# Two-unit attention steps in the second block, and new step sequences in all four mixers, in a two-block transformer kernel

## The chip, the cores and the metric

The kernel runs as one program on one core of a Trainium2 chip. The metric is device time in microseconds (us) of one execution, the median of several. TensorE (PE in the rows) multiplies; VectorE (DVE) and ScalarE (ACT) work on rows of 128 partitions; GpSimd (POOL) does little here; SyncE (SP) issues nearly all DMAs, which bring 389 MB of weights from HBM.

## The reference

One sequence of 256 tokens of width 1024, float32, goes through two different blocks of two layers each. A layer is a mixer and then a feed-forward part.

```
# first block, a layer                       # second block, a layer
h = rms_norm(x)*(1+scale)+shift              h = rms_norm(x)
proj = h @ w_in          # 1024 x 3088       proj = h @ w_in            # 1024 x 2656
a = stick_breaking_attention  # 8 heads      y_a = softmax attention, low-rank q, k, v   # 4 heads
b = gla_chunked          # 4 heads           y_b = difference of two softmaxes times v   # 4 heads
x += gate * ([a, b] @ w_out)                 y_c = banded softmax attention with sinks   # 4 heads
x += gate * (32 SwiGLU experts, 2 a token)   y_d = 4 heads with a bias table (na_rpb)
                                             x += [norm y_a, y_b, norm y_c, norm y_d] @ w_out
                                             x += relu(h @ w_up)**2 @ w_down
```

The modulation (scale, shift, gate) of the first block is `silu(c) @ w_ada`, 1024 x 6144 for each layer. In the second block every one of the four branches works on 256 x 256 scores for each head: for the rows of one half i (128 queries), score = q k^T times a scale (with a mask or bias in C and D), softmax over 256 keys, times v of 64 columns. In B the two softmaxes of a head are combined as p0/sum0 - lambda p1/sum1 before the product with v.

## The kernel before

The four mixers are called mix1 (first block, layers 0 and 1) and mix2 (second block). In the profiled execution they lie at about 38 to 194 us, 437 to 579, 825 to 966 and 1151 to 1290. The experts follow each mix1, the feed-forward part (L536, L2335) each mix2.

**Weights.** Weights come by DMA into four slots of 1 MB (`ring`). Most are split into two float32r parts, ACT writing the rounded part (L916) and DVE the rest (L925), in two halves of 1024 columns each. Every product with them is three matmuls (`parts3`). The weights of the modulation and a few small ones are used unsplit.

**Lanes.** Within a mixer each engine's program is woven from several generators, the lanes. `steps(order, *lanes)` goes through a string of digits; each digit advances the lane of that number to its next `yield`. So the string `ORDER[mixer, layer, engine]` is the order in which the engine issues its work, and nothing else decides it. An engine does its instructions in that order and waits at semaphores. A digit whose lane has ended, or is empty, does nothing.

In mix1 the lanes are 0 the projections (`pe_main1`: L516, L536, and the output projection L737), 1 the attention heads in pairs (`pe_heads` lane 0), 2 nothing, 3 the heads one at a time, 4 the gated linear attention (`pe_gla`: L820, L830 to L834, transposes L845), 5 the modulation (`pe_ada_lane`: column sums L597, and where a gate is made the product L608, to which DVE adds the bias with L625), 6 the transposes of q and k (L759). In mix2 they are 0 the projections (`pe_main2`, L1780, L1804, output L1828), 1 to 3 the attention units, 4 the rest (`pe_misc2`), and on ACT and DVE 5 and 0 for the splits and the projections' evacuation.

**Units.** There are 20 attention units in a mix2: (branch, query half i, part p), 8 of B, 4 each of A, C and D. Each has two score rows (j = 0, 1), 128 x 256 each, in one PSUM bank (2 KB a partition). They are dealt in turn to three lanes with one bank each (3, 4, 5). On PE a unit has three steps: scores S (L1850, two matmuls), transposes T of the probabilities (L1859), product V with v (L1865). Between S and T, DVE finds the row maxima (L2151) and negates and scales them (L2158), in C and D after adding mask or bias (L2149); ACT takes the exponentials, one instruction for each score row (L1992); B also divides and combines on DVE (L2165 to L2170). Between T and V, ACT copies the transposed probabilities out of PSUM (L1998). After V, DVE moves the result to `y` (L2175, L2178), which also frees the bank for the lane's next S. S of B, C and D contracts over 64 partitions or fewer: part p's operands lie in partitions 0 to 63 or 64 to 127, by p. A contracts over 96.

**Fins.** After the last unit of a branch, `pe_fin2` (L1944) transposes its normed y, ACT and DVE turn it into two parts (L2068, L2256), and the output projection L1828 of that tile can run. The order of tiles there is B, A, C, D.

## Time and profile before

| | |
|---|---|
| median of 3 runs | 1479.4 us (1476.24 to 1483.46) |
| the profiled execution | 1481.0 us, of it 1478.8 us from the first to the last instruction |
| PE busy | 1314.6 us, 89% |
| DVE busy | 730.4 us, 49% |
| ACT busy | 526.9 us, 36% |
| mean granted clock of TensorE | 0.962 of full speed |

Two kinds of stretch alternate. In the experts the DMA engines are busy all the time at 421 GB/s and PE works for about two thirds of it. In the mixers and in the second block's feed-forward part PE is busy nearly all the time and the DMA engines are not. Lines are those of the kernel before; in the listings of the changed kernel they are shifted, L1850 to L1870, L1859 to L1880, L1865 to L1888, L1804 to L1822, L1828 to L1846, L1944 to L1968.

### The profile page before, as it was taken

Reading aid. Unit: us, or ns where it says so; the run is one execution under the profiler, and the core shown is the slowest. Engines: PE = TensorE matmul, PEld = TensorE weight load, DVE = VectorE, ACT = ScalarE, POOL = GpSimd, SP = SyncE. Lnnn points to the kernel's source line nnn. Section 1 sums busy time; section 2 is a strip of 40 time slices with the busy share of each in tenths; the row PEclk is TensorE's granted clock in tenths of the full one; section 3 lists DMA queues with packets and bytes.
Section 4 is the critical chain, followed back from the end, with each engine's and each line's share of the span. In section 5 each row is a group of like instructions: output and inputs, shape, how many; then the busy total and the mean of one; then the engine's idle time right before and its main releaser. Section 6 shows DMA issues by size and latency. Waiting matters only on the chain. (4 is left out here: it accounts for less than half of the span.)

```text
span 1478.8 us, 21544 instructions
## 1 busy us (share of the span) xinstructions
PE 1314.6 (89%) x9066; PEld 981.4 (66%) x9066; DVE 730.4 (49%) x1126; ACT 526.9 (36%) x894; POOL 50.7 (3%) x46
## 2 busy tenths in 40 slices
PE   5999998766579999976666999999999999999997
PEld 2765674433247667633432778789898878799986
DVE  1744653121146467321111777765555777764554
ACT  3535331000044354200000546654444546644343
POOL 0200000000002000000000110000000110000000
PEclk9999999888899999998887999999999999999999
DMA  9798799999977957999999714456555305455551
GB/s 353 284 334 308 280 413 421 421 421 420 399 283 275 341 200 301 421 421 421 421 393 402 179 32 172 142 156 202 186 193 173 107 3 198 143 168 189 186 198 43
DMA packets 135976, 392.10 MB, mean 265 GB/s; under 512 B 26816, under 2 KB 40128, under 8 KB 111296
## 3 DMA queue, kind: packets, MB, share of 16 engines
q1 hardware_dynamic: 132128, 389.48, 70.7%
q10 hardware_dynamic: 3744, 1.15, 0.4%
q8 instruction: 76, 1.25, 0.3%
q14 instruction: 28, 0.23, 0.0%
HBM read 389.45 MB, written 1.05 MB: 264 GB/s over the span
## 5 line engine op out<-in xcount | busy, mean ns | idle before, releaser
L413 DVE TENSOR_TENSOR spl<-ring,spl 128x2048 fp32r<-128x2048 f32 x65 | 149.3, 2297 | 135.7 <-ACT spl L404 135.7
L536 PEld LDWEIGHTS ps<-hh,spl 128*128 128x128 f32 x1728 | 204.1, 189 | 6.9 <-issue 5.8
L536 PE MATMUL ps<-hh,spl 128*128 128x256 f32 x1728 | 206.2, 280 | 2.8 <-DVE hh L499 2.8
L404 ACT ACTIVATE spl<-ring 128x2048 fp32r<-128x2048 f32 x66 | 126.7, 1920 | 148.3 <-PE ps L536 107.7
L2335 PE MATMUL ps<-spl,ur 128*128 128x512 f32 x768 | 176.7, 389 | 0.0
L2335 PEld LDWEIGHTS ps<-spl,ur 128*128 128x128 f32 x768 | 143.2, 188 | 29.2
L925 DVE TENSOR_TENSOR spl<-ring,spl 128x1024 fp32r<-128x1024 f32 (+2 forms) x120 | 138.4, 1175 | 24.6 <-ACT spl L916 24.2
L1337 PE MATMUL ps<-ring,ar 128*32 128x256 f32 x928 | 98.5, 443 | 57.4 <-issue 25.0
L1337 PE MATMUL ps<-spl_as_slots,ar 128*32 128x256 f32 x864 | 103.8, 479 | 45.1 <-DMA spl_as_slots<-in_w_up 29.3
L916 ACT ACTIVATE spl<-ring 128x1024 fp32r<-128x1024 f32 (+2 forms) x120 | 116.8, 1011 | 49.4 <-DMA ring<-in_w_out 11.7
L516 PE MATMUL ps<-spl,hh 128*128 128x512 f32 x480 | 117.6, 398 | 3.8 <-DVE spl L925 1.3
L1550 DVE TENSOR_TENSOR ar<-ps,ar 128x256 f32<-128x256 f32 x16 | 6.8, 425 | 223.9 <-ACT ar L1426 223.9
L1337 PEld LDWEIGHTS ps<-ring,ar 128*32 128x32 f32 x928 | 49.9, 127 | 93.5 <-issue 82.3
L516 PEld LDWEIGHTS ps<-spl,hh 128*128 128x128 f32 x480 | 88.4, 188 | 32.1 <-issue 12.3
L1426 ACT ACTIVATE ar<-ps 128x256 f32<-128x256 f32 x16 | 6.2, 385 | 283.6 <-PE ps L1337 283.6
L1337 PEld LDWEIGHTS ps<-spl_as_slots,ar 128*32 128x32 f32 x864 | 51.7, 136 | 70.1 <-issue 62.2
L1804 PE MATMUL ps<-hh,spl 128*128 128x256 f32 (+1 forms) x672 | 85.9, 286 | 3.0 <-DVE hh L499 2.9
L1804 PEld LDWEIGHTS ps<-hh,spl 128*128 128x128 f32 (+1 forms) x672 | 81.6, 192 | 7.0 <-issue 4.1
L597 PE MATMUL ps<-ring,ccol 128*32 128x512 f32 x384 | 53.4, 652 | 18.0 <-DMA ring<-in_w_ada 15.7
L1382 PE MATMUL ps<-spl_as_slots,ar 128*32 128x512 f32 x400 | 58.1, 594 | 10.6 <-ACT ar L1439 6.6
L1402 PE MATMUL ps<-gate,hh_as_floats 128*128 128x512 f32 x128 | 63.0, 614 | 1.9 <-ACT hh_as_floats L1435 1.7
L1329 PE MATMUL ps<-ar,xn 128*128 128x256 f32 (+1 forms) x320 | 58.3, 340 | 0.0
(370 smaller groups left out, 1758.5 us busy)
## 6 DMA issues: line engine op xcount, KB each, us to landing
ring<-in_w_up SPq DMA_DIRECT2D x52, 1024.0 KB, 5.3
spl_as_slots<-in_w_down SPq DMA_DIRECT2D x50, 1024.0 KB, 15.4
ring<-in_w_ada SPq DMA_DIRECT2D x48, 1024.0 KB, 7.2
spl_as_slots<-in_w_up SPq DMA_DIRECT2D x40, 1024.0 KB, 17.4
ring<-in_w_gate SPq DMA_DIRECT2D x38, 1024.0 KB, 16.8
ring<-in_w_down SPq DMA_DIRECT2D x38, 1024.0 KB, 4.9
ring<-in_w_in SPq DMA_DIRECT2D x34, 1024.0 KB, 7.5
ring<-in_w_out SPq DMA_DIRECT2D x16, 1024.0 KB, 6.9
```

The source lines that it names most:

```text
L404: sc.activation(t.hi, t.raw, ACT.Copy).then_inc(s_hi, 2)
L413: v.tensor_tensor(t.lo, t.raw, t.hi, ALU.subtract).then_inc(s_lo, 1)
L516: ins = pe.matmul(ps[:, banks[i], 0:cn], le, ri, start=(kk == 0 and q == 0), stop=(kk == 7 and q == 2), skip_group_check=True)
L536: ins = pe.matmul(ps[:, banks[m // 2], (m % 2) * 256:(m % 2) * 256 + 256], le, ri, start=(kk == 0 and q == 0 and m % 2 == 0), stop=(kk == ...
L916: sc.activation(t.hi[:, h], t.raw[:, h], ACT.Copy).then_inc(s_hi, 1)
L925: ins = v.tensor_tensor(t.lo[:, h], t.raw[:, h], t.hi[:, h], ALU.subtract)
L1329: ins = pe.matmul(slots_out(c, k), xn[:, i, 128 * k:128 * k + 128], mo.pr[:, i, s0:s0 + n], start=(i == 0), stop=(i == 1), skip_group_chec ...
L1337: ins = pe.matmul(ps[32 * j:32 * j + 32, 2 + q % 2, 256 * z:256 * z + 256], mo.xg[:, e // 16, k, 32 * (e % 16):32 * (e % 16) + 32], T[("ga ...
L1382: ins = pe.matmul(ps[32 * j:32 * j + 32, c, :], mo.aT[q % 2][:, f, 32 * j:32 * j + 32], T["down", l, 4 * q + j].raw[:, f, 512 * c:512 * c ...
L1402: pe.matmul(ps[:, 6 + m % 2, :], mo.pT[:, q, 128 * i:128 * i + 128], mo.ys[:, 512 * c:512 * c + 512], start=True, stop=True).then_inc(s_b, 1)
L1804: ins = pe.matmul(o, le, ri, start=(kk == 0 and q == 0 and m % 2 == 0), stop=(kk == 7 and q == 2), skip_group_check=True)
L2335: ins = pe.matmul(ps[:, 2 * cc + i, :], le, ri, start=(d == 0 and f2 == 0 and f == 0 and q == 0), stop=(d == 7 and f2 == 1 and f == 1 and ...
```

## The change

The three unit lanes of mix2 become two. Lane 1 has seven double units, each of both parts of one branch and half (two of B's four), with two PSUM banks (3 and 4). Lane 3 (bank 5) has six single units. Together they hold the same 20 parts. A double unit's instructions are the same matmuls and exponentials, one for each part; what DVE and ACT can do over both parts at once becomes one instruction of twice the width: the maxima (1024 columns instead of 512), the small operations on sums, C's mask, the copy after T and the evacuation after V. In B's combination and D's bias there is still one instruction for each part. The score matmuls are written with j outside and the part a inside, so that neighbours lie in different halves of the partitions.

```diff
-        UNITS = [Unit(br, i, p) for br, n in (("B", 4), ("A", 2), ("C", 2), ("D", 2)) for p in range(n) for i in range(2)]
...
-                self.b, self.units = 3 + z, UNITS[z::3]
...
-        LANES = [Lane(z) for z in range(3)]
+        LANES = [Lane(0, units_of(("B", 0, (0, 1)), ("B", 1, (0, 1)), ("B", 0, (2, 3)), ("A", 0, (0, 1)), ("C", 0, (0, 1)), ("D", 0, (0, 1)),
+                                  ("D", 1, (0, 1)))),
+                 Lane(1, units_of(("B", 1, (2,)), ("B", 1, (3,)), ("A", 1, (0,)), ("A", 1, (1,)), ("C", 1, (0,)), ("C", 1, (1,))))]
...
-                for j, (q, k) in enumerate(u.qk):
-                    ins = pe.matmul(ps[:, L.b, 256 * j:256 * j + 256], q, k, start=True, stop=True)
+                for j in range(2):
+                    for a in range(len(u.ps)):
+                        q, k = u.qk[a][j]
+                        ins = pe.matmul(ps[:, L.b + a, 256 * j:256 * j + 256], q, k, start=True, stop=True)
...
-                for j in range(2):
-                    ins = sc.activation(L.pt[:, j, :], src[:, j, :], ACT.Exp, bias=sm[:, j:j + 1], scale=1.0 if masked else u.scale,
-                                        accum_out=sm[:, 2 + j:3 + j])
+                for a in range(L.n):
+                    for j in range(2):
+                        m = 2 * a + j
+                        ins = sc.activation(L.pt[:, a, j, :], src[:, a, j, :], ACT.Exp, bias=top[:, m:m + 1], scale=1.0 if masked else u.scale,
+                                            accum_out=total[:, m:m + 1])
...
+                elif u.br == "D":
+                    for a, p in enumerate(u.ps):
+                        ins = v.scalar_tensor_tensor(L.pt[:, a, :, :], src[:, a, :, :], scale, na_bias(p, u.i), ALU.mult, ALU.add)
...
-                v.wait_ge(*own_dve(v.tensor_reduce(sm[:, 0:2], src, AX.X, ALU.max)))
+                v.wait_ge(*own_dve(v.tensor_reduce(pair(top), src, AX.X, ALU.max)))
```

All strings of `ORDER` are new, those of mix1 too, where nothing else changes and where the digit 2 is gone:

```diff
-ORDER = {("mix1", 0, "PE"): "004004000665505005566501525301535005650051255345025314542012513215205054351045551040454250152550054420030040005", ...
+ORDER = {("mix1", 0, "PE"): "00400400550506655050505660355540515053505401543505515305531003550414555415410055140150004400000", ...
```

What SP and POOL issue, and its order, stays. The places below are those on which the prediction rests.

**PE, end of mix1 layer 0.** L608 makes a half of a gate, L597 is the next column sum of the modulation, L737 the output projection. Before:

```order
105 L597 MATMUL ps<-ring,ccol 32x512 x4
106 L516 MATMUL ps<-spl,hh 128x512 x12
107 L608 MATMUL ps<-ar,cst 128x512
108 L597 MATMUL ps<-ring,ccol 32x512 x8
109 L737 MATMUL ps<-spl,ur 128x512 x24
```

Changed:

```order
86 L608 MATMUL ps<-ar,cst 128x512
87 L831 MATMUL ps<-xn,ar 128x256
88 L834 MATMUL ps<-ar,xn 128x128 x2
89 L831 MATMUL ps<-xn,ar 128x256
90 L834 MATMUL ps<-ar,xn 128x128 x2
91 L860 MATMUL ps<-ar 128x256 x2
92 L863 MATMUL ps<-ar 128x128 x2
93 L516 MATMUL ps<-spl,hh 128x512 x24
94 L597 MATMUL ps<-ring,ccol 32x512 x8
```

The column sum that stood right behind the gate's product now has other matmuls between.

**PE, middle of mix2 layer 0**, from the last units of B to the first of A. Changed:

```order
1167 L1880 MATMUL ps<-cst,xn 128x128 x4
1168 L1888 MATMUL ps<-ar,xn 128x64 x4
1169 L1870 MATMUL ps<-ar 128x256 x2
1170 L1870 MATMUL ps<-gate,ar 128x256 x2
1171 L1822 MATMUL ps<-hh,spl 128x256 x24
1172 L1935 MATMUL ps<-ar,ring 64x256 x4
1173 L1822 MATMUL ps<-hh,spl 128x256 x24
1174 L1940 MATMUL ps<-ring,ar 128x256 x2
1175 L1880 MATMUL ps<-cst,xn 128x128 x4
1176 L1870 MATMUL ps<-ar 128x256 x2
1177 L1888 MATMUL ps<-ar,xn 128x64 x4
1178 L1870 MATMUL ps<-ar 128x256 x4
```

In rows 1167 to 1169 T, V and the next S of lane 1 stand directly behind one another, and in 1177 and 1178 V and the next S again. Before, in the same place, steps of other lanes stood between two steps of one lane:

```order
1174 L1804 MATMUL ps<-hh,spl 128x256 x12
1175 L1865 MATMUL ps<-ar,xn 128x64 x2
1176 L1859 MATMUL ps<-cst,ar 128x128 x2
1177 L1859 MATMUL ps<-cst,xn 128x128 x2
1178 L1850 MATMUL ps<-ar 128x256
1179 L1850 MATMUL ps<-gate,ar 128x256
1180 L1804 MATMUL ps<-hh,spl 128x256 x24
```

**PE, end of mix2 layer 1**, the last units, of D. Before:

```order
1350 L1850 MATMUL ps<-ar 128x256 x2
1351 L1865 MATMUL ps<-ar,xn 128x64 x4
1352 L1859 MATMUL ps<-cst,ar 128x128 x4
1353 L1828 MATMUL ps<-spl,hh 128x512 x12
1354 L1865 MATMUL ps<-ar 128x64 x4
1355 L1859 MATMUL ps<-cst,xn 128x128 x4
```

Changed:

```order
1315 L1870 MATMUL ps<-ar 128x256 x4
1316 L1846 MATMUL ps<-spl,ur 128x512 x12
1317 L1968 MATMUL ps<-cst,gate 128x128 x4
1318 L1880 MATMUL ps<-cst,xn 128x128 x8
1319 L1846 MATMUL ps<-spl,hh 128x512 x12
1320 L1888 MATMUL ps<-ar,xn 128x64 x8
```

Row 1315 is S of the last double unit and 1318 its T; between them stand 12 matmuls of the output projection and one fin. It is the same in layer 0.

## Rows read from the trace of the kernel before

**Rows 1.** Windows: the mixers and two short stretches; us busy (instructions), clock, DMA.

```profile
core 0: us, PE busy (x) PEld busy (x) DVE busy (x) ACT busy (x) POOL busy (x), PEclk, DMA share, GB/s
38.40:193.60 155.20, 150.28 (x833) 103.82 (x834) 89.15 (x132) 67.71 (x98) 12.49 (x8) 0.99 0.86 308
167.10:170.50 3.40, 3.40 (x15) 1.09 (x8) 2.76 (x4) 2.78 (x3) 0.00 (x0) 0.50 0.38 108
437.50:579.00 141.50, 140.49 (x770) 101.94 (x771) 88.02 (x126) 66.84 (x96) 12.45 (x8) 1.00 0.75 266
824.70:966.40 141.70, 139.38 (x873) 117.77 (x874) 106.23 (x214) 72.84 (x184) 12.01 (x9) 0.98 0.41 126
880.50:883.90 3.40, 3.40 (x16) 2.98 (x15) 3.26 (x6) 1.21 (x4) 2.68 (x2) 0.50 0.00 0
1151.00:1290.40 139.40, 136.55 (x873) 115.09 (x874) 107.67 (x214) 76.15 (x186) 11.08 (x9) 1.00 0.37 119
```

**Rows 2.** Timeline of PE, mix1 layer 0: start, us, line, [idle before <-releaser].

```profile
109.45 2.96 PE L516 MATMUL ps<-spl,hh 128*128 128x512 f32 x12 [1.34 <-DVE spl L925]
113.43 1.06 PE L597 MATMUL ps<-ring,ccol 128*32 128x512 f32 x8 [1.02 <-DMA ring<-in_w_ada]
...
163.10 1.02 PE L608 MATMUL ps<-ar,cst 128*128 128x512 f32 x2
166.45 3.06 PE L597 MATMUL ps<-ring,ccol 128*32 128x512 f32 x16 [2.33 <-DVE gate L625]
```

**Rows 3.** Timeline of PE, pieces of mix1 layer 1 and of mix2 layer 1.

```profile
479.87 0.70 PE L860 MATMUL ps<-ar 64*128 64x256 f32 x4
480.40 0.39 PE L863 MATMUL ps<-ar 64*128 64x128 f32 x4
...
489.38 0.70 PE L860 MATMUL ps<-ar 64*128 64x256 f32 x2
489.92 0.38 PE L863 MATMUL ps<-ar 64*128 64x128 f32 x2
...
1184.31 0.70 PE L1850 MATMUL ps<-ar 64*128 64x256 f32 x2
1184.85 0.59 PE L1850 MATMUL ps<-gate,ar 64*128 64x256 f32 x2
1185.37 0.61 PE L1889 MATMUL ps<-ar 32*32 32x256 f32 x2
...
1243.73 0.61 PE L1859 MATMUL ps<-cst,ar 128*128 128x128 f32 x4
```

**Rows 4.** Waits of PE in mix2 layer 1: us in total, times, longest.

```profile
PE ps L1944 <- DVE gate L2178: 0.6, 1, 0.6
PE ps L1865 <- ACT ar L1998: 0.5, 1, 0.5
PE ps L1859 <- DVE xn L2170: 0.2, 1, 0.2
```

**Rows 5.** Timeline of mix2 layer 1, one unit of D from S to the exponentials.

```profile
1266.04 1.13 PE L1850 MATMUL ps<-ar 64*128 64x256 f32 x4
1267.29 0.69 DVE L2149 SCALAR_TENSOR_TENSOR ar<-ps,ar 128x512 f32<-128x512 f32 x1 [0.84 <-PE ps L1850]
1268.73 0.17 DVE L2158 TENSOR_SCALAR st<-st 128x2 f32<-128x2 f32 x1
1268.94 0.51 ACT L1992 ACTIVATE ar<-ar,st 128x256 f32<-128x256 f32 x1 [0.84 <-DVE st L2158]
```

**Rows 6.** Groups of instructions: busy us, mean ns of one, idle before.

```profile
L1065 DVE TENSOR_REDUCE st<-ar 128x16 f32<-128x1024 f32 x2 | 2.4, 1220 | 2.7 <-ACT ar L944 2.7
L2151 DVE TENSOR_REDUCE st<-ps 128x2 f32<-128x512 f32 x12 | 8.2, 686 | 1.7 <-PE ps L1850 1.6
L916 ACT ACTIVATE spl<-ring 128x1024 fp32r<-128x1024 f32 x18 | 18.5, 1054 | 1.3 <-PE ps L1828 1.3
L1998 ACT ACTIVATE xn<-ps 128x512 f32<-128x512 f32 x8 | 4.8, 594 | 4.2 <-PE ps L1859 4.2
```

**Rows 7.** Timeline of mix2 layer 1: the last V, its evacuation and the fin behind it.

```profile
1280.20 1.00 PE L1865 MATMUL ps<-ar,xn 128*128 128x64 f32 x8
1281.23 0.29 DVE L2178 TENSOR_TENSOR gate<-ps,st 128x128 f32<-128x128 f32 x1 [0.80 <-PE ps L1865]
1281.78 0.63 PE L1944 MATMUL ps<-cst,gate 128*128 128x128 f32 x4 [0.58 <-DVE gate L2178]
```

**Rows 8.** Timeline of PE, the same 96 matmuls at the start of mix2 in layer 0 and layer 1.

```profile
824.78 12.79 PE L1804 MATMUL ps<-hh,spl 128*128 128x256 f32 x96 [2.24 <-DVE hh L499]
1151.12 11.18 PE L1804 MATMUL ps<-hh,spl 128*128 128x256 f32 x96 [0.62 <-DVE hh L499]
```

More of the change, by code:

```diff
@@ L1738, in program, with __init__ @@
-        LANES = [Lane(z) for z in range(3)]
+            def __init__(self, z, units):
+                self.b, self.units, self.n = 3 + 2 * z, units, 2 - z
+                n = self.n
+                self.sm = [st[:, 160 + 24 * z + 2 * n * q:160 + 24 * z + 2 * n * q + 2 * n] for q in range(6)]
+                pt, ptT = ((xn[:, 0, :], xn[:, 1, :]) if z == 0 else (carve(5632, 512), carve(7424, 512)))
+                self.pt = pt.rearrange("p (a j b) -> p a j b", j=2, b=256)
+                self.ptT = ptT.rearrange("p (a j b c) -> p a j b c", j=2, b=2, c=128)
+                self.ptTw = ptT.rearrange("p (a n) -> p a n", n=512)
+                self.banks = ps[:, self.b:self.b + n, :]
+                self.scores = self.banks.rearrange("p a (j n) -> p a j n", n=256)
+                self.psum, self.scalar, self.vector = p_ln[z], a_ln[z], v_ln[z]
@@ new lines, in units_of, with pair @@
+        def units_of(*parts):
+            return [Unit(br, i, p) for br, i, p in parts]
+        LANES = [Lane(0, units_of(("B", 0, (0, 1)), ("B", 1, (0, 1)), ("B", 0, (2, 3)), ("A", 0, (0, 1)), ("C", 0, (0, 1)), ("D", 0, (0, 1)),
+                                  ("D", 1, (0, 1)))),
+                 Lane(1, units_of(("B", 1, (2,)), ("B", 1, (3,)), ("A", 1, (0,)), ("A", 1, (1,)), ("C", 1, (0,)), ("C", 1, (1,))))]
+        def pair(sm):
+            return sm.rearrange("p (a j) -> p a j", j=2)
@@ L1856, in pe_units @@
                     pe.wait_ge(L.scalar, 2 * at + 1)
-                for j in range(len(u.vs)):
-                    for kt in range(2):
-                        ins = pe.transpose(ps[:, L.b, 256 * j + 128 * kt:256 * j + 128 * kt + 128], L.pt[:, j, 128 * kt:128 * kt + 128], ident)
+                for a, vs in enumerate(u.vs):
+                    for j in range(len(vs)):
+                        for kt in range(2):
+                            ins = pe.transpose(ps[:, L.b + a, 256 * j + 128 * kt:256 * j + 128 * kt + 128], L.pt[:, a, j, 128 * kt:128 * kt + 128],
+                                               ident)
                 ins.then_inc(L.psum, 1)
@@ L1862, in pe_units @@
                 pe.wait_ge(L.scalar, 2 * at + 2)
[L1863 to L1865 removed]
+                for a, vs in enumerate(u.vs):
+                    for j, c in enumerate(vs):
+                        for kt in range(2):
+                            ins = pe.matmul(ps[:, L.b + a, 64 * j:64 * j + 64], L.ptT[:, a, j, kt, :], m2.v[:, kt, c:c + 64], start=(kt == 0),
+                                            stop=(kt == 1))
                 ins.then_inc(L.psum, 1)
@@ L1953, in pe_mix2 @@
                 pe_spin(pe, 6, 2)
-            steps(ORDER["mix2", l, "PE"], pe_main2(pe, g, l), *(pe_units(pe, l, L) for L in LANES), pe_misc2(pe, l))
+            steps(ORDER["mix2", l, "PE"], pe_main2(pe, g, l), pe_units(pe, l, LANES[0]), iter(()), pe_units(pe, l, LANES[1]), pe_misc2(pe, l))
         def act_main2(sc, l):
@@ L2079, in act_mix2 @@
             act_hT(sc, g, PR(f"n1{l}"), last, 1)
-            steps(ORDER["mix2", l, "ACT"], act_split(sc, last), *(act_units(sc, l, L) for L in LANES), act_misc2(sc, l), act_main2(sc, l))
+            steps(ORDER["mix2", l, "ACT"], act_split(sc, last), act_units(sc, l, LANES[0]), iter(()), act_units(sc, l, LANES[1]), act_misc2(sc, l), act_main2(sc, l))
             for c in range(2):
@@ L2274, in dve_mix2 @@
             dve_hT(v, g, PR(f"n1{l}"), last, 1)
-            steps(ORDER["mix2", l, "DVE"], dve_split(v, last), *(dve_units(v, l, L) for L in LANES), dve_misc2(v, l), dve_main2(v, l))
+            steps(ORDER["mix2", l, "DVE"], dve_split(v, last), dve_units(v, l, LANES[0]), iter(()), dve_units(v, l, LANES[1]), dve_misc2(v, l), dve_main2(v, l))
             v.wait_ge(s_used, T["out2", l, 2].m + 1)
```

116 lines of the change are left out of this document (62 added, 54 removed), and 6 rows, old and new, of the table ORDER.

## The prediction

> **What bounds the kernel now.** I read the windows first, stage by stage [rows 1]. All that the change touches lies in the four mixers, and in them PE is the limit: it is busy for 150.3 of 155.2 us, 140.5 of 141.5, 139.4 of 141.7 and 136.6 of 139.4. DVE (89 to 108 us) and ACT (67 to 76) have time to spare, so that fewer of their instructions gain nothing by themselves. A gain must come from PE's waits, from PE working on fewer passes one after another, or from the clock. The windows bound the first: the waits of the four mixers are 4.9, 1.0, 2.3 and 2.8 us, 11.0 in all. Next I read in PE's timeline where they are, and how many passes a score step takes.
>
> **Mix1, layer 0.** The largest wait of all is 2.33 us at 166.45: the column sum L597 needs the PSUM bank that L625 on DVE still reads, and it stands directly behind the product L608 that L625 waits for [rows 2]. Changed, that sum stands behind 4 L834, two L831, one pair of heads and 24 L516, some 8 us of PE work, against the 3.35 us from L608's start to the sum's start in the trace. So this wait goes: -2.3. Right behind it the granted clock is 0.50 for 3.4 us, the lower level, 1.2 GHz [rows 1], and the 16 passes of L597 take 3.06 us, where 8 take 1.06 [rows 2]; that is about 1.0 more there, and somewhat more in the L737 behind. What PE did before it: it stood still for those 2.33 us. I take -1.6 with it (bounds 0 and -1.7, half of 3.4). The waits of 1.34 (splits of a late tile) and 1.02 (a tile of modulation weights) [rows 2] come from DMA at 0.86 of its capacity over the stage; the new sequence consumes the same tiles in the same load order, and I leave half of them: -1.2. New waits: L820 stands three times with only about 2 us between (6 us before), and each needs four small DVE operations on the state; I take +1.0 (0 to 2.5). The new place of the last column sums is covered. Sum: -4.1, with the bounds -6.0 and 0.
>
> **Does it reach the end?** Behind this stage the experts run at the DMA's full rate, and one could think that the gain drowns there. The DMA runs at 0.86 in the stage because it waits for slots that PE and the splits free; if these come 4 us earlier, so does all that is queued behind. I let it pass whole except for 0.6. So -3.5.
>
> **Mix1, layer 1.** 1.0 us of waits in all [rows 1]. The new sequence keeps the same neighbours by and large; -0.4, bounds -0.9 and +1.5.
>
> **Mix2, what PE saves.** A score step of a unit (two matmuls in float32, two passes each, hence x4) holds PE from 1184.31 to 1185.37, 1.06 us [rows 3]. Two matmuls whose operands lie in different halves of the partitions run side by side: in mix1 the pair of heads (x4 in L860, x4 in L863) is through in 0.85 us, and a single head (x2, x2) in the same 0.85 [rows 3]. In a double unit of B, C or D the parts lie in different halves, in A they don't (96 partitions). So six of the seven double units save one step of 1.06 us, 6.4 us in a mixer. Against this, the kernel before already has neighbours of this kind: three units' steps stand together at the start of B, and in layer 1 two more in C and D. I take off 1.3 in layer 0 and 2.1 in layer 1: PE saves **5.1 and 4.3 us**. T and V, over 128 partitions, keep their time. If the pairs should not run side by side with two banks as outputs, this is zero; the heads of mix1 write two banks too, so I hold that unlikely.
>
> **Mix2, what PE waits for instead.** With three lanes there were 1.3 to 2.3 us of waits inside each mixer, the longest 0.6 [rows 4]. With two lanes a lane's next step comes sooner, and a double unit takes longer on the way. I price its ways from single rows:
> - S to T in D: 0.2 to reach DVE (S ends about 1267.1, L2149 starts at 1267.29); two L2149 of 0.69; the maxima over 1024 columns 1.22 [rows 5, 6]; L2158 0.2; four exponentials at one in 0.5 us, 1.9; 0.1 back: **5.1 us**. A needs 3.7, B (with its combination) 5.9.
> - T to V: 0.2, a copy of 1024 columns 1.05, 0.05: **1.3 us**; of 512 columns 0.85 [rows 6]. No copy of 1024 out of PSUM is in the trace; L916 of that width is the nearest row, and twice 0.594 the upper bound, 1.4.
> - V to the next S of the lane: 0.74, as from the end of the last V (1281.04) to L1944 at 1281.78 [rows 7]; 0.9 where the evacuation is wider.
>
> Then I add up the PE work that stands between (1.06 a score step, 0.22 a transpose, 2.8 for 12 L1828) and take the difference where it is short. Layer 0: T, V and S of the second double unit of B directly behind each other 0.8 + 0.7; V to S into A 0.9; T to V of A's single unit, directly behind, 0.95; S of A's second single unit, whose evacuation stands behind a split on DVE, 1.1; the fin of B and the first S of A 0.3; T to V of D's first double unit 0.4; V to S of its second 0.9; S to T of the last one, 5.1 against the 3.2 of the fin and 12 L1828 between them, **1.9**; the end as now 0.8. Together 8.7, against 2.3. Layer 1 is laid out more loosely: V to S in B 0.7, S to T in B and A 1.2, V to S in A 0.3, D 0.4 + 0.1 + 1.9, the end and small ones 1.3: 5.9 to 7, against 2.8, so +3.8. So the mixers come to -5.1 + 6.4 = **+1.3** and -4.3 + 3.8 = **-0.5**. Bounds of each: all waits but the 1.9 covered, -3.5; every way longer by a split of 1.2 us in between at three more places, +5.
>
> The Trainium skill bears on this (TensorEngine Tiling (Array Packing), Performance Considerations, PSUM Bottleneck): packing speeds up the matmuls but not the evacuation of PSUM, which may become the bottleneck. By the packing alone the second block would gain the whole 9.4 us; by this rule the gain is spent on waits for ACT and DVE. My ways worked out from the rows side with the rule.
>
> **The clock in mix2.** The same 96 matmuls take 12.79 us in layer 0 and 11.18 in layer 1 [rows 8], and at 880.5 the clock is again 0.50 for 3.4 us although PE was busy all the time [rows 1]. Each such stretch costs up to 1.7. New waits of 1.9 us may bring one more, other positions may spare one; I leave the sum as it is and let the range have 1.7 on both sides. The Trainium skill says the same (TensorE: Matmul & The Clock Gate, Part 1): the point at which the clock changes depends on how the work happens to lie, from run to run.
>
> **Sum.** -3.5 - 0.4 + 1.3 - 0.5 = -3.1 us, against 1481.0 of the profiled execution (span 1478.8 and 2.2 around it): 1477.9. That execution is 1.6 above the median of the three runs, 1479.4; on the median the forecast is **1476 us**.
>
> **Rivals.**
> - The ways are covered (chance 0.22). The waits of mix2 stay at their 5.1 us and the packing pays in full: -9.4 - 3.9 gives **1466**. For it: DVE and ACT lose the fixed cost of many small instructions, the maxima 2 x 686 against 1220 ns [rows 6]. Against it: the last S to T is 1.9 short whatever DVE does.
> - The gain of mix1 is lost, to late tiles or in the experts, and mix2 comes out even (0.20): **1480**.
> - Slower (0.13): the long uninterrupted work of a double unit on DVE (D: 1.38 + 1.22 in a row) stands ahead of the splits L925, and PE's projections wait for their tiles, which they never do inside mix2 now. It decides from about 0.9 us at each of the 12 tiles of a mixer; 1 us at each, in both mixers, is +24, of which some replaces the waits counted above: at half of the tiles +10 to 12, **1487**.
> - The forecast (0.45).
>
> **How the numbers follow.** About 0.5%, 7.4 us, is what a measurement of this kernel can tell from no change: faster is below 1472.0, slower above 1486.8. Faster: the first rival and a fifth of the forecast, 0.31. Slower: half of the last rival and a bit, 0.08. The rest, 0.61, is no change. The range runs from 1466, the first rival, to 1483, with which the upper bounds of the forecast are in and most of the slower rival is out.
>
> **What would show it.** In mix1 layer 0 no wait for L625 at L597, and the stage (38.4 to 193.6) shorter by 3 to 5 us. In mix2, score steps of double units with x8 in about 1.06 us; if they take 2.1, the packing failed and the time is near 1486. A wait of about 1.9 us at the last T of lane 1 in both layers, waits of 0.7 to 1 at V and S of the double units, and stages of 139 to 144 us. If PE's waits in each stay below 3 us, the first rival is right. What would make it wrong altogether is a change outside of the mixers: the experts' stretches should keep their lengths to 2 us.

## The result, and the profile after

The changed kernel takes **1493.0 us** (median of 4 runs, 1489.6 to 1495.1), the kernel before 1479.3: a ratio of 1.0084, with an interval of 1.0065 to 1.0103. It is slower by 0.8%, where the forecast was 1476 with a range up to 1483. The profiled execution is the fastest of the four, 1489.6 us, span 1487.5; that of before took 1481.0. These two traces differ by 8.7 us of span, less than the 12.4 us that the ratio gives, so one pair of traces does not hold the whole loss.

The windows of the changed kernel, the mixers first, in the form of [rows 1]:

```profile
core 0: us, PE busy (x) PEld busy (x) DVE busy (x) ACT busy (x) POOL busy (x), PEclk, DMA share, GB/s
38.10:191.90 153.80, 149.19 (x831) 102.60 (x832) 88.72 (x131) 67.36 (x97) 12.50 (x8) 1.00 0.85 305
436.80:579.50 142.70, 138.90 (x768) 101.25 (x769) 87.81 (x126) 66.36 (x95) 12.82 (x8) 1.00 0.74 260
825.90:972.50 146.60, 137.62 (x872) 116.28 (x873) 98.77 (x179) 71.27 (x173) 10.47 (x9) 0.95 0.39 121
1157.50:1298.80 141.30, 135.40 (x872) 113.80 (x873) 99.75 (x179) 73.45 (x175) 12.29 (x9) 0.98 0.37 118
...
903.90:907.30 3.40, 3.40 (x13) 2.60 (x12) 3.12 (x8) 1.27 (x5) 0.00 (x0) 0.50 0.99 384
...
955.10:958.50 3.40, 3.40 (x10) 2.53 (x9) 1.41 (x2) 1.08 (x3) 0.00 (x0) 0.50 0.00 0
1211.10:1217.90 6.80, 6.42 (x29) 5.40 (x29) 3.19 (x5) 1.53 (x7) 6.04 (x5) 0.50 0.00 0
```

From here on a mixer's length is counted from the start of its first projection matmul to the start of its last matmul of the output product. In the trace of before these lengths are 154.9, 141.2, 141.4 and 139.0 (the windows of [rows 1] are 0.3 to 0.4 wider). Against them the four mixers of the changed kernel are 1.0 shorter, 1.6 longer, 5.2 longer and 2.3 longer; the experts behind mix1 are 0.6 and 0.3 longer, the start is 0.4 shorter, and the rest the same. So the loss in this trace is in mix2. PE is busy there for hardly less than before (137.6 against 139.1, 135.4 against 136.3 on the same bounds), although it does fewer passes one after another. The column of the granted clock says why: 0.95 and 0.98, where [rows 1] has 0.98 and 1.00. Four stretches of 3.4 us in layer 0 and one of 6.8 in layer 1 ran at the lower level, 0.50; before there were two of 3.4 (from 825.9 and from 880.5) and none.

The waits of PE in mix2 layer 0, in the form of [rows 4] (for one line waiting for another: us in total, times, longest):

```profile
PE ps L1846 <- DVE hh L2293: 2.9, 2, 2.7
PE ps L1888 <- ACT ar L2025: 2.8, 1, 2.8
PE ps L1822 <- DVE hh L499: 2.2, 1, 2.2
PE ps L1888 <- ACT xn L2025: 1.0, 2, 0.7
PE ps L1870 <- DVE gate L2211: 0.8, 2, 0.4
```

(The one of 2.2 lies ahead of the stage.) With the shorter ones that are left out here, the waits come to 9.0 us in the stage (146.6 less 137.6), where 2.3 had been; in layer 1 to 5.9, where 2.8 had been. The two long ones, in the timeline of PE, with two rows of ACT for the first:

```profile
899.15 0.60 PE L1880 MATMUL ps<-cst,ar 128*128 128x128 f32 x4
899.63 2.00 ACT L916 ACTIVATE spl<-ring 128x1024 fp32r<-128x1024 f32 x2 [1.54 <-DMA ring<-in_w_in]
901.97 0.58 ACT L2025 ACTIVATE ar<-ps 128x512 f32<-128x512 f32 x1
902.60 1.10 PE L1888 MATMUL ps<-ar 128*128 128x64 f32 x8 [2.84 <-ACT ar L2025]
903.54 0.76 PE L1968 MATMUL ps<-cst,gate 128*128 128x128 f32 x4
904.24 2.08 PE L1870 MATMUL ps<-ar 96*128 96x256 f32 x4
...
948.25 2.08 PE L1870 MATMUL ps<-ar 64*128 64x256 f32 x8 [0.52 <-DVE gate L2214]
950.26 1.11 PE L1968 MATMUL ps<-cst,gate 128*128 128x128 f32 x4
954.05 4.57 PE L1846 MATMUL ps<-spl,hh 128*128 128x512 f32 x12 [2.67 <-DVE hh L2293]
```

At 902.60 V (L1888) of A's first single unit stands directly behind its T (L1880). Its copy L2025 could start at 899.8, when T ends, but ACT has two weight splits and two steps of the fin of B ahead of it, and the splits had themselves waited 1.54 us for a DMA. At 954.05 the output product needs L2293 of the fin of C, which stands on DVE behind the bias and the maxima of the last double unit. At the lower clock matmuls take up to twice their length: L1870 at 904.24, behind the first wait, takes 2.08 us where it takes 1.10 at full clock, and around the second wait L1870 at 948.25 takes 2.08 where it takes 1.13, and 12 L1846 take 4.57 where they take 2.99 a little later. At the second place the clock had fallen at 948.2, before the wait of 2.67 us began.

What the double units were to bring is there. Four rows of the changed kernel, score steps of a double and of a single unit of C and D, in mix2 layer 1:

```profile
1245.66 1.13 PE L1870 MATMUL ps<-ar 64*128 64x256 f32 x8
1246.73 3.10 PE L1798 MATMUL ps<-spl,hh 128*128 128x256 f32 x24
...
1254.35 1.13 PE L1870 MATMUL ps<-ar 64*128 64x256 f32 x4
1255.41 3.00 PE L1846 MATMUL ps<-spl,ur 128*128 128x512 f32 x12
```

Eight passes or four, the next instruction starts 1.06 to 1.07 us later. A's double unit is the comparison: its parts take 96 partitions each and can't lie in different halves, and there eight passes take 1.99 us.

```profile
897.32 1.99 PE L1870 MATMUL ps<-ar 96*128 96x256 f32 x8 [0.38 <-DVE gate L2211]
```

### The profile page after: what moved, and what is told of

Read it like the earlier page. It is cut to its first block, busy times and chain, and to the rows that moved or that the text cites. A ratio compares the mean times of both kernels' runs of the same rounds, so it can differ in the third digit from the quotient of the medians.

```text
span 1487.5 us, 21416 instructions
## 1 busy us (share of the span) xinstructions
PE 1313.9 (88%) x9066; PEld 978.3 (66%) x9066; DVE 715.6 (48%) x1056; ACT 523.4 (35%) x878; POOL 50.8 (3%) x46
## 3 DMA queue, kind: packets, MB, share of 16 engines
HBM read 389.45 MB, written 1.05 MB: 263 GB/s over the span
## 4 chain that ended last, share of the span: by engine, by line
PE 71%; DMA 20%; DVE 4%; ACT 3%; issue 1%; ACTq 0%; SPq 0%; POOL 0%; DVEq 0%
PE ps L536 13%; PE ps L2372 12%; DMA spl_as_slots<-in_w_up 8%; PE ps L1337 6%; PE ps L1822 5%; PE ps L516 5%; PE ps L1382 4%; DMA spl_as_slots<-in_w_down 4%; PE ps L1846 3%; DMA ring<-in_w_in 3%; DMA ring<-in_w_ada 3%; PE ps L1329 2%; PE ps L1402 2%; PE ps L737 2%; PE ps L1798 2%; PE ps L1888 2%
## 5 line engine op out<-in xcount | busy, mean ns | idle before, releaser
L925 DVE TENSOR_TENSOR spl<-ring,spl 128x1024 fp32r<-128x1024 f32 (+2 forms) x120 | 139.2, 1182 | 31.1 <-ACT spl L916 30.7
L1337 PE MATMUL ps<-spl_as_slots,ar 128*32 128x256 f32 x864 | 106.9, 496 | 45.5 <-DMA spl_as_slots<-in_w_up 28.8
L516 PE MATMUL ps<-spl,hh 128*128 128x512 f32 x480 | 118.7, 399 | 2.4 <-DVE hh L1038 1.3
L516 PEld LDWEIGHTS ps<-spl,hh 128*128 128x128 f32 x480 | 88.3, 188 | 32.1 <-issue 11.3
L1822 PE MATMUL ps<-hh,spl 128*128 128x256 f32 (+1 forms) x672 | 86.0, 287 | 2.9 <-DVE hh L499 2.9
L1822 PEld LDWEIGHTS ps<-hh,spl 128*128 128x128 f32 (+1 forms) x672 | 81.7, 192 | 7.2 <-issue 4.8
L597 PE MATMUL ps<-ring,ccol 128*32 128x512 f32 x384 | 52.4, 640 | 17.7 <-DMA ring<-in_w_ada 16.2
## 6 DMA issues: line engine op xcount, KB each, us to landing
spl_as_slots<-in_w_up SPq DMA_DIRECT2D x40, 1024.0 KB, 17.1
```

Source lines behind the costliest of these rows:

```text
L516: ins = pe.matmul(ps[:, banks[i], 0:cn], le, ri, start=(kk == 0 and q == 0), stop=(kk == 7 and q == 2), skip_group_check=True)
L925: ins = v.tensor_tensor(t.lo[:, h], t.raw[:, h], t.hi[:, h], ALU.subtract)
L1337: ins = pe.matmul(ps[32 * j:32 * j + 32, 2 + q % 2, 256 * z:256 * z + 256], mo.xg[:, e // 16, k, 32 * (e % 16):32 * (e % 16) + 32], T[("ga ...
L1822: ins = pe.matmul(o, le, ri, start=(kk == 0 and q == 0 and m % 2 == 0), stop=(kk == 7 and q == 2), skip_group_check=True)
```

## The experiments

Twelve kernels were run, each also timed against the kernel before (6 to 12 runs each, 25 to 35 of before). "Half" is the time at half clock (1.2 GHz) in the stage of the one trace, from the granted clock; lengths are in us, counted as above. Each row has one trace, and the same sequences give lengths of a stage that differ by more than 3 us from trace to trace (mix2 layer 0 of the changed kernel, e1, e3 and e5: 146.6 to 150.0; mix1 layer 0 as before: 151.8 to 154.9).

| run | median, us | ratio to before (interval) | mix1 l0 | mix1 l1 | mix2 l0 (half) | mix2 l1 (half) |
|---|---|---|---|---|---|---|
| before | 1479.3 to 1481.4 | | 154.9 | 141.2 | 141.4 (6.8) | 139.0 (0) |
| changed | 1493.0 | 1.0084 (1.0065 to 1.0103) | 153.8 | 142.7 | 146.6 (13.7) | 141.3 (6.8) |
| e1 mix2 only | 1487.1 | 1.0043 (1.0023 to 1.0064) | 154.1 | 141.1 | 148.1 (17.1) | 141.7 (6.8) |
| e2 mix1 only | 1485.7 | 1.0044 (1.0027 to 1.0060) | 154.4 | 144.2 | 142.1 (6.8) | 140.6 (3.4) |
| e3 parts outside | 1494.1 | 1.0093 (1.0065 to 1.0122) | 154.8 | 143.1 | 148.1 (17.1) | 141.7 (6.8) |
| e4 eased | 1488.1 | 1.0056 (1.0033 to 1.0078) | 154.6 | 144.5 | 139.8 (0) | 141.1 (6.8) |
| e5 head first | 1494.3 | 1.0082 (1.0063 to 1.0102) | 154.4 | 144.4 | 150.0 (20.3) | 141.1 (6.8) |
| e6 mix1 l0 only | 1482.9 | 1.0013 (0.9999 to 1.0027) | 153.7 | 141.0 | 143.1 (6.8) | 139.2 (0) |
| e7 waits put in | 1482.5 | 1.0016 (1.0001 to 1.0030) | 151.8 | 141.1 | 141.8 (3.4) | 140.3 (0) |
| e8 combined | 1484.7 | 1.0031 (1.0017 to 1.0045) | 154.7 | 143.4 | 138.8 (0) | 140.1 (0) |
| e9 mix2 moved | 1482.7 | 1.0016 (0.9998 to 1.0035) | 151.9 | 141.0 | 138.8 (0) | 140.7 (3.4) |
| e10 moved, mix1 l1 | 1481.1 | 1.0000 (0.9981 to 1.0019) | 152.7 | 139.9 | 142.0 (6.8) | 139.8 (0) |
| e11 middle moved | 1490.5 | 1.0055 (1.0031 to 1.0079) | 155.4 | 142.9 | 142.8 (3.4) | 138.9 (0) |
| e12 more waits | 1487.3 | 1.0037 (1.0014 to 1.0060) | 153.3 | 141.4 | 139.9 (3.4) | 142.2 (0) |

Where a row has the same sequences as another in a stage, it is a repeat of that stage.

### Which half of the change costs what: e1, e2, e6

e1 is the changed kernel with the strings of mix1 of before; e2 is the kernel before with the strings of mix1 of the changed one; e6 has only those of mix1 layer 0.

```diff
 # e1, on the changed kernel (and so for layer 1, ACT and DVE)
-ORDER = {("mix1", 0, "PE"): "00400400550506655050505660355540515053505401543505515305531003550414555415410055140150004400000", ...
+ORDER = {("mix1", 0, "PE"): "004004000665505005566501525301535005650051255345025314542012513215205054351045551040454250152550054420030040005", ...
```

> The changed kernel with the mix1 sequences of the kernel before, so that only mix2 differs from it. Theory (the loss lies in mix2: 6.7 us of new waits and 6.9 us more at half clock in layer 0, 3.1 and 6.8 in layer 1, against some 9 us saved by the packing): 1479 + 5.2 + 2.3 = about 1487 by the profiled stages, and if the other changed runs' lower clock (0.950 to 0.954) belongs to mix2 too, up to 1492. Rival (mix1's new sequences cost what the medians show beyond that): 1480 to 1483.

> The kernel before with the mix1 sequences of the changed one. Theory: mix1 layer 0 is 1.0 us shorter, layer 1 1.6 longer (a new wait of 2.8 us), the experts within 1: 1479 to 1481, no change. My prediction's step was -3.9, 1475. Rival (the median's loss lies here): 1486 or more.

> The kernel before with the changed sequences of mix1 layer 0 alone. My prediction's step was -3.5. Theory now (the mixer is 0.5 to 1 us shorter, but at its end 0.67 MB less has landed, which the experts at 421 GB/s give back as 1.6 us): 1479.5 to 1481.5. Then the rest of the +6.3 that both layers of mix1 cost comes from layer 1, +4 to +6 with its wait and its half clock.

By the ratios e1 costs 6.4 us and e2 6.5, together 12.9, and the whole change 12.4: the two halves add up. e1 bears out what was expected. e2 does not: 1485.7 where 1479 to 1481 was expected. I had reckoned with the one trace of the changed kernel, whose mix1 layer 1 (142.7, nothing at half clock) is shorter than in the four other traces with the same sequence there (142.9 to 144.5). e6 puts 1.9 of the 6.5 on layer 0 (-0.1 to +4.0 by its interval), which leaves about 4.6 for layer 1, a difference of two medians and as rough. The traces show less for layer 1: with its new sequences the stage is 143.5 us long on average (five traces, without e5, e8 and e10, which move steps in it) against 141.1 with the old ones (six), 2.4 more.

**Layer 0.** The wait of L597 for L625 is gone, as forecast: it is in all seven traces with the old sequences (0.8 to 2.8 us) and in none of the seven with the new ones. The one for L925 is gone as well. PE's waits in the changed kernel:

```profile
68.35 1.06 PE L597 MATMUL ps<-ring,ccol 128*32 128x512 f32 x8 [0.95 <-DMA ring<-in_w_ada]
87.08 1.07 PE L597 MATMUL ps<-ring,ccol 128*32 128x512 f32 x8 [0.51 <-DMA ring<-in_w_ada]
98.66 1.06 PE L597 MATMUL ps<-ring,ccol 128*32 128x512 f32 x8 [1.37 <-ACT gate L604]
112.56 1.13 PE L810 MATMUL ps<-ar 128*128 128x256 f32 x4 [1.10 <-DVE xn L1131]
137.00 1.07 PE L597 MATMUL ps<-ring,ccol 128*32 128x512 f32 x8 [0.39 <-DMA ring<-in_w_ada]
```

4.3 us at five places, where [rows 2] have 4.7 at three. Over all traces the stage did not get shorter: it takes 151.8 to 154.9 us with the old sequence (seven traces, mean 153.3) and 153.7 to 155.4 with the new one (seven, mean 154.4). The pair of before and changed, 154.9 and 153.8, is by chance the other way round.

And less has landed at its end. The stretch from 160 us to the stage's end, in the kernel before and then in the changed one:

```profile
160.00:193.30 33.30, 30.96 (x139) 22.58 (x136) 23.94 (x31) 15.81 (x24) 1.64 (x1) 0.95 0.83 314
```

```profile
160.00:191.90 31.90, 31.90 (x155) 25.66 (x152) 24.51 (x31) 16.09 (x25) 1.64 (x1) 1.00 0.66 248
```

Counted from the DMA packets of the traces, 60.9 to 61.0 MB have landed when the stage ends with the old sequence and 60.3 MB with the new one, in all seven traces of each. At 160 us it is the other way round, 50.6 to 51.1 MB against 52.5: the new sequence is ahead until then and loses it in the last 30 us. The experts, at 421 GB/s, need about 1.6 us for the 0.66 MB that lack (an estimate from these two numbers); from the stage's end to the start of the next mixer it is 244.7 us on average with the old sequence and 246.0 with the new one. Both parts together: mix1 layer 1 begins at 434.4 to 437.6 us with the old sequence (mean 436.2) and at 436.6 to 440.4 with the new one (mean 438.5), 2.3 us later, which agrees with e6.

### Does the packing need the interleaved order: e3

```diff
-                for j in range(2):
-                    for a in range(len(u.ps)):
+                for a in range(len(u.ps)):
+                    for j in range(2):
                         q, k = u.qk[a][j]
```

> The changed kernel with the score matmuls of a double unit in the order part outside, row j inside, so that only the middle two of the four lie in different halves of the partitions one behind the other. If neighbours in different halves really run side by side, a double S of B, C or D takes about 1.6 us instead of 1.1, twelve of them in two mixers: +6.4 us of PE work, of which the waits right behind take up some: 1496 to 1499. Rival (packing does not pay, or not here): same as the changed kernel, 1493, and S takes the same time.

The time is that of the changed kernel, as the rival had it, but not for its reason: the step is as short as with the parts interleaved, and that is half of the 1.99 us that eight passes take without different halves.

```profile
1249.99 1.14 PE L1870 MATMUL ps<-ar 64*128 64x256 f32 x8
1251.06 3.10 PE L1798 MATMUL ps<-spl,hh 128*128 128x256 f32 x24
```

It is 1.07 us to the next instruction, with both matmuls of one half ahead of both of the other. So the packing works in either order, and the interleaving that the change writes for it is not what brings it. How the matmuls come to overlap the traces don't show.

### Moving steps in mix2: e4, e11, e8, e9

e4 moves steps of layer 0 at two places: on ACT in the middle (and on DVE, in keeping, L2214 ahead of a split L925), and on PE at the end (there one split on DVE and two on ACT move behind the last unit's exponentials, since they would wait for the slot that the moved product frees):

```diff
 # ACT, middle
-L916 ACTIVATE spl<-ring 128x1024 x2
 L2076 ACTIVATE st<-st 128x8
 L2078 ACTIVATE st<-st 128x8
 L2025 ACTIVATE ar<-ps 128x512
 L2019 ACTIVATE xn,st<-ps,st 128x256 x4
+L916 ACTIVATE spl<-ring 128x1024 x2
 # PE, end
-L1846 MATMUL ps<-spl,ur 128x512 x12
 L1880 MATMUL ps<-cst,xn 128x128 x8
...
 L1870 MATMUL ps<-ar 128x256 x4
 L1968 MATMUL ps<-cst,gate 128x128 x4
+L1846 MATMUL ps<-spl,ur 128x512 x12
```

> The changed kernel with steps of mix2 layer 0 moved at two places: on ACT the copy of A's single unit and the fin of B ahead of two weight splits, and at the end the output projection's second half of tile 1 behind the score step of the last double unit. The waits of 2.84 and 2.67 us should shrink to about 1.2 and 0.2 in place of them, -4 us. Theory (the stretches at half clock follow these waits): two of four stretches of 3.4 us go as well, -3.4: mix2 layer 0 from 146.6 to about 139 to 141, total 1486. Rival (the clock falls by chance or by something else): only the waits go, layer 0 at 142 to 143.5, total 1489.

The stage falls by 6.8 us, to 139.8, shorter than before the change. Its window:

```profile
829.30:969.10 139.80, 131.88 (x871) 112.04 (x872) 98.66 (x179) 71.36 (x173) 10.48 (x9) 1.00 0.41 127
```

The waits are 7.9 us, only 1.1 less, since one of 2.87 us came up in place of the first (the two splits now stand ahead of L2095, the fin's evacuation on ACT, and L1950 has to wait until L2293 behind it has read the bank). The rest of the gain, 5.7 us of busy time, is the clock: no stretch at half clock is left. So the length followed the theory and the reason did not: the stretches went although a wait of the same length stayed. And one of the four, 57 us into the stage, lies ahead of everything that e4 moves (the first moved step comes about 72 us into it), so not all of the 5.7 us can be put down to the move. The whole kernel came out at 1488.1, 2 us above the theory's 1486.

```profile
905.09 1.04 PE L1880 MATMUL ps<-cst,xn 128*128 128x128 f32 x8
909.00 1.12 PE L1950 MATMUL ps<-ar 128*128 128x512 f32 x2 [2.87 <-DVE ur L2293]
909.56 3.30 PE L1822 MATMUL ps<-hh,spl 128*128 128x256 f32 x24
```

e11 has the middle's move alone, with one more: L2095 between the two splits, which takes the 2.87 down to 1.74.

> The changed kernel with only the first of the two moves of the eased one: in the middle of mix2 layer 0, ACT's copy of A's unit and the fin of B ahead of the splits. If each stretch at half clock belongs to the waits just ahead of it, the one about 78 us into the stage goes, and the ones about 123 and 130 us into it, behind the last double unit, stay (6.8 us): stage at 143 to 144.5, total 1489 to 1491. If one wait has to do with all, or none with any: 0 or 13.7 us of it.

In its trace the wait at the end is longer than ever, and yet the clock stays up around it. The only stretch at half clock in its mix2 is at the start of layer 0, 1.2 us in.

```profile
950.42 1.13 PE L1870 MATMUL ps<-ar 64*128 64x256 f32 x8 [0.52 <-DVE gate L2214]
951.49 0.66 PE L1968 MATMUL ps<-cst,gate 128*128 128x128 f32 x4
955.27 2.98 PE L1846 MATMUL ps<-spl,hh 128*128 128x512 f32 x12 [3.13 <-DVE hh L2293]
```

Its 12 runs lie in two groups, four at 1483.2 to 1486.7 with the profiled one at 1486.9, and seven at 1489.8 to 1493.3. The same instructions in the same order, then, take 1483 or 1493 us. Mix2 layer 1, where e11 and the changed kernel are the same, shows one possible reason: 6.8 us at half clock in five traces and none in this one. That is worth up to 3.4 of the 10 us; what the rest is isn't shown.

```profile
1157.10:1296.00 138.90, 132.68 (x872) 111.47 (x873) 100.31 (x179) 73.43 (x175) 12.35 (x9) 1.00 0.37 120
```

e8 puts all moves together, with 12 L1822 between T and L1930 in layer 1 and, in mix1, the old sequence of layer 0 and e5's of layer 1; e9 has all of mix1 as before, and the 12 L1822 one step later:

```diff
 # PE, mix2 layer 1, e9
 L1888 MATMUL ps<-ar,xn 128x64 x4
+L1822 MATMUL ps<-hh,spl 128x256 x12
 L1870 MATMUL ps<-ar 128x256 x2
 L1870 MATMUL ps<-gate,ar 128x256 x2
-L1822 MATMUL ps<-hh,spl 128x256 x36
+L1822 MATMUL ps<-hh,spl 128x256 x24
```

> All together: two-part units; mix1 layer 0 as before; mix1 layer 1 changed and with the head's step first on DVE; mix2 layer 0 with the moved steps of the eased kernel, but L2095 between the two splits, so that L1950 no longer waits 2.9 us; mix2 layer 1 with 12 L1822 between the transposes and L1930, where 6.8 us at half clock lay. Theory: 154.9, 139.9, 137 to 140, 137.5 to 138.5 in the four mixers: total 1472 to 1475, faster than the kernel before. Rival (the double units only turn packing into waits and a lower clock, wherever the steps stand): 1479 or more.

> Both mix1 layers as in the kernel before; the double units; mix2 layer 0 with the moved steps of the combined kernel; mix2 layer 1 with 12 L1822 between the last V before and the next S of lane 1 (not ahead of L1930, where the combined kernel turned it into a wait of 1.66 us for L2250). Theory: mixers of about 154.5, 141.1, 138.8 and 137.5 to 139, no or one stretch at half clock in mix2: 1475 to 1478, faster than the kernel before by 0.1 to 0.3%. Rival: 1480 or more, the double units bring nothing even with the waits and the clock seen to.

Both came out on the rival's side, at 1484.7 and 1482.7. In layer 0 both have 138.8 us and no time at half clock, 2.6 less than before the change. But that gain is the clock's: the five traces of the old order, less half of their time at half clock, come to 138.0 to 140.1 us (an estimate from the table). At full clock, then, the double units show no gain over the single ones: the 4.0 us of PE's work that they save come back as waits (6.7 us in e8 and e9, 2.3 before). And the feed-forward part behind is 0.8 us longer in e8, e9 and e10 (185.8 against 185.0 in all others), for a reason that isn't shown. In layer 1 they have 140.1 and 140.7: the moved L1822 brought a wait of 1.66 and of 1.13 us for L2250, and e9 still has 3.4 us at half clock. And a profile is one execution: these two are among the three shortest of their kernels (1481.2 and 1479.9).

### Mix1 layer 1: e5, e10

In the changed kernel L870 waits 2.83 us for L1188, which stands on DVE behind L636, and that waits for a DMA: among DVE's waits at that place the first is

```profile
DVE aff L636 <- DMA ada_moved_columns<-gate: 7.0, 1, 7.0
```

```diff
 # DVE, e5
+L1186 SCALAR_TENSOR_TENSOR ar<-ps,ar 128x384
+L1188 TENSOR_TENSOR ar<-ar,cst 128x2x128
 L636 TENSOR_REDUCE aff<-ada_moved_columns 128x8
...
-L1186 SCALAR_TENSOR_TENSOR ar<-ps,ar 128x384
-L1188 TENSOR_TENSOR ar<-ar,cst 128x2x128
```

> The changed kernel with one step moved: on DVE in mix1 layer 1 the modulation's step, which waits 7 us for a DMA, stands behind the head's mask step L1186 and a split, no longer ahead of them. The wait of 2.83 us of L870 for L1188 should go. Theory (time at half clock, which three of four profiles with these sequences show right behind this wait, goes as well): mix1 layer 1 from 142.7 (no half clock in that profile) or 144.2 (6.8 us of it) to 139.5 to 140.5, total 1488 to 1490. Rival (only the wait goes, or another step inherits it): 1490 to 1493.

The wait went and another of the same length came, the rival's way:

```profile
514.67 1.23 PE L860 MATMUL ps<-ar 64*128 64x256 f32 x4 [2.81 <-DVE ur L1191]
```

L1191 needs L1013 on ACT, and ahead of that stood a split which had waited 7.1 us for its tile and started at 512.8. e10 is e9 with the changed sequences of mix1 layer 1, e5's step, and on ACT this L1013 ahead of the split.

> The same with the changed sequences in mix1 layer 1, and there the head's steps ahead of the DMA's on both engines: on DVE L1186 ahead of the modulation's step, on ACT L1013 of lane 1 ahead of a weight split whose tile lands late. The waits of L870 and of L860 go. Theory (the tile of w_in itself comes late, because its slot was freed late, so the wait only moves on to L516, for L925): mix1 layer 1 at 143 to 144.5 and the total 2 to 3 us above e9. Rival (the two orders were the cause): 139.5 to 140.5, total 1 us below e9.

The theory of a late tile fell: nothing of the wait moved on to L516. The stage is 139.9 us, 1.2 shorter than with the old sequence, with one wait of 1.31 us inside. e8 has the same mix1 but for the step on ACT, and 143.4 us. So in this stage the change had been good for a gain and lost 3 us by two steps that stood behind waits for DMAs; each of these numbers is from one trace. The whole kernel is at 1481.1, equal to before (0.998 to 1.002), and it is the best version of the twelve; none is faster than the kernel before.

### Waits put into the kernel before: e7, e12

```diff
-                sc.activation(L.ptT.rearrange("p a b c -> p (a b c)")[:, 0:w], ps[:, L.b, 0:w], ACT.Copy).then_inc(L.scalar, 1)
+                pieces = 16 if l == 1 and L.b == 5 and n in (1, 3) else 1      # e12: 32
+                for c in range(0, w, w // pieces):
+                    e = c + w // pieces
+                    ins = sc.activation(L.ptT.rearrange("p a b c -> p (a b c)")[:, c:e], ps[:, L.b, c:e], ACT.Copy)
+                ins.then_inc(L.scalar, 1)
```

> The kernel before, with the copy L1998 of two units in mix2 layer 1 (one of B, one of A) made in 16 narrow pieces instead of one, so that V waits for ACT about 3 us at each of two places, with nothing else changed. That stage had no time at half clock. The waits: +5 to +6 us. If waits of this size bring the lower clock: 3.4 to 6.8 us at half clock as well, mix2 layer 1 from 139.0 to 146 or 148, total +7 to +9. If the clock falls for other reasons: 144 to 145, total +5 to +6.

> The kernel before with the copy L1998 of the same two units of mix2 layer 1 as in e7, but in 32 pieces instead of 16 (there only one wait of 1.4 us had come, and no half clock). Now waits of about 4.5 and 2 to 3 us. By the waits alone: mix2 layer 1 from 140.3 to 145.5 to 147. If waits of this size bring the lower clock, 3.4 to 6.8 us of it and 147.5 to 150.

The pieces are shorter than I took them for (32 of 8 columns in 2.35 us), so that the waits were 1.42 in e7, and 2.43 and 0.99 in e12:

```profile
1212.66 0.66 PE L1865 MATMUL ps<-ar 128*128 128x64 f32 x4 [2.43 <-ACT ar L2001]
...
1246.04 1.10 PE L1865 MATMUL ps<-ar 128*128 128x64 f32 x8 [0.99 <-ACT ar L2001]
```

The stage is 1.3 and 3.2 us longer than in the trace of before, and neither trace shows time at half clock in it. e7 is inconclusive for the question, its waits being small. In e12 the trace speaks for the waits alone, but it is of one of the shortest executions (1481.3): by the ratio of all its runs (1478.0 to 1493.5) it costs 5.5 us, 2.3 more than the stage in the trace. Those runs have the mean clock of before (0.956 and 0.957), so what the other 2.3 are isn't shown.

## Why the prediction was wrong

**The steps that failed.** The forecast was a change of -3.1 us, and the two halves cost +6.5 (e2) and +6.4 (e1). The larger miss is in mix1: forecast -3.9, shown +6.5, 10.4 us off. It has two steps. One is "Does it reach the end?", the -3.5 of layer 0; the other is "keeps the same neighbours by and large; -0.4" for layer 1. With these two as forecast, the time would have been about 1483. The other miss, 5.6 us, is in mix2: forecast +0.8, shown +6.4. Its largest part is the step "I leave the sum as it is and let the range have 1.7 on both sides", since the clock did not stay as it was.

The split of mix2 in the two profiled executions follows. PE's busy time without half clock is 132.68 in layer 1 (e11) and 131.88 in layer 0 (e4); the old order has no trace of layer 0 without it, so I take e12's 137.58 less half of its 3.4 us, 135.9:

| mix2, us | forecast l0 | trace l0 | forecast l1 | trace l1 |
|---|---|---|---|---|
| PE's work at full clock | -5.1 | -4.0 | -4.3 | -3.6 |
| waits | +6.4 | +6.7 | +3.8 | +3.1 |
| the clock | 0 | +2.5 | 0 | +2.7 |
| sum | +1.3 | +5.2 | -0.5 | +2.3 |

- **PE's work.** That a double score step with its parts in different halves takes the time of a single one was right; 1.1 and 0.7 us of the 9.4 are missing. The price of six steps of 1.06 was right, so I probably took off too little for the pairs that the kernel before already had; that is argued, not shown.
- **The waits.** The sum was right within 0.7 us, the places not all, and that is in part luck. S to T of the last unit in layer 1 takes 5.04 us (1275.82 to 1280.86), priced at 5.1, the maxima over 1024 columns 1.22 and the copy of 1024 columns 1.02, priced at 1.05. But the order at the end of layer 0 is not that of layer 1, as I had taken it: there the fin stands directly behind S, and the 12 L1846 that need the fin's result stand behind it and ahead of T. So these wait for L2293, 2.67 us, and T doesn't wait at all. And V of A's first single unit waits 2.84, priced at 0.95, because I counted the copy and not what ACT has queued ahead of it. The waits that I had priced at A's second single unit and at D did not come, or were shorter, and made up for it. The price of V to S used 1281.04 as the end of a V that by [rows 7] ends at 1281.20; it is 0.58 and not 0.74, which changes little.
- **The clock.** Layer 0 with the changed sequences has 13.7, 17.1, 17.1 and 20.3 us at half clock in four traces; with the old ones 6.8, 6.8, 6.8, 3.4 and 3.4 in five. Layer 1 has 6.8 in five of six, against 0 in four and 3.4 in one. On average that is 11.6 and 5 us more, worth up to half of it, 8.3 us. The range had allowed 1.7 either way; what came is several times that, and on one side.
- **Mix1, layer 0, and whether its gain reaches the end.** The wait for L625 went as forecast, but it was dear by luck in the one trace that I had: over the seven traces with the old sequence it is 1.8 us on average and not 2.3, and time at half clock stands behind it in three of them. I left 1.2 us of the old waits and took +1.0 for new ones; what is there in the changed kernel comes to 4.3. Over all traces the stage is 1.1 us longer, not 4.1 shorter. "If these come 4 us earlier, so does all that is queued behind" failed too: less has landed at the end of the stage, since the DMA engines are less busy in its last 30 us (share 0.66, 0.83 before). Forecast -3.5, shown +1.9 by e6 (-0.1 to +4.0) and +2.3 by the start of the next mixer.
- **Mix1, layer 1.** "Keeps the same neighbours by and large" was true of PE alone. On DVE and ACT two steps of the heads had come to stand behind steps that wait for a DMA, 2.8 and 1.0 us of waits in the trace. Forecast -0.4 with +1.5 as the bound, shown about +4.6 by the medians (e2 less e6) and +2.4 by the stage in the traces.
- **The range.** It was said to hold the upper bounds of the forecast. They are 3.5, 1.9, 3.7 and 5.5 us above the four terms, which would reach about 1491, and the range ended at 1483.

Of the rivals, the slower one had a time near the truth (1487) by a mechanism that didn't happen: no projection of mix2 waits for L925 in the changed kernel. "The gain of mix1 is lost" did happen, and more than that. The Trainium skill's rule that packing does not speed up the evacuation of PSUM, which may become the bottleneck (TensorEngine Tiling (Array Packing), PSUM Bottleneck), agrees with the trace by its outcome: 7.6 us of work saved, 9.8 us of new waits, nearly all for ACT and DVE. But the two longest, 2.84 and 2.67 us, are there because of what the engines had queued ahead, not because an evacuation takes long (0.58 us for the copy, 0.87 for the two L2293).

**What stays open** is what makes the granted clock fall. The places say something. With the changed order, stretches of layer 0 lie at 78 to 79, 122 to 124 and 129 to 130 us into the stage in three traces, and at 82 and 130 in the fourth (e5). None of the five traces with moved steps has any there, and none of the old order. But e11 lost the later ones with only the middle moved, and 2.87 and 3.13 us of standing still were followed by full clock in e4 and e11, so no single wait decides it. Other stretches are in the old order too, or follow no wait. One begins within 1.3 us of layer 0's start, in nine of the fourteen traces, old order and new. Another, also in nine of both kinds, begins 54 to 62 us into layer 0, and the one of 6.8 us in layer 1 begins 53 us in. These two stand behind the same small matmuls, and PE need not have stood still ahead of them: it was busy for all of the 10.5 us before 880.5 in the kernel before, and for 10.93 of the 11.0 us before 1211 in the changed one.

```profile
1208.88 1.91 PE L1930 MATMUL ps<-ar 32*32 32x256 f32 x8
```

Whether these small matmuls bring the lower clock was not tested, and they don't always: e11 has the same ones in the same order in layer 1, with PE busy for 9.92 of 10 us, and stays at full clock. Nor is it settled by the order: e10 has e9's sequences in mix2 and 6.8 us in layer 0, where e9 has none, and none in layer 1, where e9 has 3.4.

## What to carry to other kernels

When an order is written out by hand, price each moved step with what its own engine has queued ahead of it, waits for DMAs above all, and not by its duration alone; two such steps undid the gain in mix1 layer 1, and moving them gave 3 us back. Merging units to save passes on PE takes away the slack between dependent steps; here the waits took back all that the packing saved, and in most orders a lower clock came on top. A stage that ends ahead of a DMA-bound one is to be judged by the bytes that have landed at its end as well, not by its own length alone. And a wait in one trace is one draw: the wait that the forecast wanted to remove is 0.8 to 2.8 us in seven traces of the same sequence.
